# The first loads in another order, the last sums begun from alpha x, and the register loads and branches around the expert pass moved

## The reference, cut to what matters

```python
q, k, v, z, xbc, dt = jnp.split(x @ w_in, IN_SPLITS, axis=-1)      # mixer; w_in is 1024 x 3080, dt its last 8 columns
x = _layer_norm(alpha * x + mixer(x), g, b)
x = _layer_norm(alpha * x + cross_attention(x, memory), g, b)
out = jnp.zeros_like(x)                                            # layer 1: _moe
for e in range(N_EXPERTS):
    out = out + _swiglu(x, w_exp_gu[e], w_exp_down[e]) * gate[..., e:e + 1]
x = _layer_norm(alpha * x + out, g, b)                             # the last norm; its x is the output
```

## Time and profile before

| what | value |
|---|---|
| time, median of 3 runs | 1843.98 us (1843.71 to 1846.29) |
| the profiled execution's own time | 1844.95 us |
| its span | 1843.2 us |
| PE busy | 1783.9 us, 97% of the span |
| DVE, ACT, POOL busy | 1223.8, 853.3, 100.2 us |
| granted TensorE clock, mean | 0.988 |
| bytes moved, mean rate | 454.10 MB, 246 GB/s |

### The profile page before, as it was taken

How to read it: one execution, slowest core, us unless ns; L and a number is a source line. 1 busy time by engine, 2 the same in 40 slices (tenths; PEclk the granted TensorE clock), 3 DMA queues, 4 the chain that set the end, 5 groups by cost and what they waited for, 6 DMA issues and landing times.

```text
span 1843.2 us, 24556 instructions
## 1 busy us (share of the span) xinstructions
PE 1783.9 (97%) x9058; PEld 1399.0 (76%) x9058; DVE 1223.8 (66%) x1708; ACT 853.3 (46%) x978; POOL 100.2 (5%) x114
## 2 busy tenths in 40 slices
PE   7999999999999999999899999999999999999996
PEld 4646587799998565577688888888888888888884
DVE  2686526155544287534438889797988889897972
ACT  1122211054432131312126777776767777777752
POOL 0530000000000531000000000000000000000000
PEclk8999999999999999999999999999999999999998
DMA  9556545845426265543766899898999999998930
GB/s 322 173 195 217 212 170 196 283 150 181 168 99 220 102 221 177 213 186 134 268 201 205 301 314 381 293 368 308 354 345 323 358 317 368 308 375 299 362 158 26
DMA packets 298982, 454.10 MB, mean 246 GB/s; under 512 B 10710, under 2 KB 213648, under 8 KB 298886
## 3 DMA queue, kind: packets, MB, share of 16 engines
q1 hardware_dynamic: 294022, 440.47, 69.6%
q0 software_dynamic: 2576, 8.38, 1.5%
q10 hardware_dynamic: 2304, 4.20, 0.6%
HBM read 440.77 MB, written 12.38 MB: 246 GB/s over the span
## 4 chain that ended last, share of the span: by engine, by line
PE 87%; DVE 6%; ACT 4%; issue 1%; SPq 1%; DMA 1%; ACTq 0%; POOL 0%; DVEq 0%
PE bank L1147 85%; PE bank L1151 2%; DVE arena L2591 1%; DVE ring_low L2074 1%; ACT high L1702 1%; ACT L1702 0%; ACT arena L1765 0%; DVE R L2205 0%; ACT xT L1801 0%; DMA out<-mem_rows 0%; ACT ye_high L1738 0%; ACT SQ L1786 0%; DVE st L2563 0%; SPq L717 0%; SPq L723 0%
## 5 line engine op out<-in xcount | busy, mean ns | idle before, releaser
L2074 DVE TENSOR_TENSOR ring_low<-ring,high 128x2048 fp32r<-128x2048 f32 x264 | 602.8, 2290 | 93.7 <-ACT high L1702 85.5
L1702 ACT ACTIVATE high<-ring 128x2048 fp32r<-128x2048 f32 x264 | 505.6, 1918 | 107.1 <-PE bank L1147 106.1
L1147 PE MATMUL bank<-high,xg_high 128*128 128x512 f32 x704 | 281.8, 400 | 7.3 <-DVE ring_low L2074 7.0
L1147 PE MATMUL bank<-ring_low,xg_high 128*128 128x512 f32 x704 | 275.1, 391 | 0.0
L1147 PE MATMUL bank<-high,xg_low 128*128 128x512 f32 x704 | 274.3, 390 | 0.0
L1147 PEld LDWEIGHTS bank<-high,xg_high 128*128 128x128 f32 x704 | 132.2, 188 | 34.0 <-DVE ring_low L2074 8.4
L1147 PEld LDWEIGHTS bank<-ring_low,xg_high 128*128 128x128 f32 x704 | 132.1, 188 | 28.6
L1147 PEld LDWEIGHTS bank<-high,xg_low 128*128 128x128 f32 x704 | 132.5, 188 | 25.2
L1765 ACT ACTIVATE arena<-bank 128x512 f32<-128x512 f32 (+3 forms) x95 | 46.3, 525 | 212.5 <-PE bank L1147 142.9
L1147 PE MATMUL bank<-high,he_high 128*128 128x512 f32 x352 | 139.7, 397 | 0.0
L1147 PE MATMUL bank<-ring_low,he_high 128*128 128x512 f32 x352 | 137.4, 390 | 0.0
(11 more groups left out here) (320 smaller groups left out, 2583.1 us busy)
## 6 DMA issues: line engine op xcount, KB each, us to landing
ring<-in_w_exp_gu SPq DMA_DIRECT2D x176, 1024.0 KB, 11.3
ring<-in_w_exp_down SPq DMA_DIRECT2D x40, 2048.0 KB, 14.0
ring<-in_w_in SPq DMA_DIRECT2D x12, 2048.0 KB, 11.3
ring<-in_w_ffn_gu SPq DMA_DIRECT2D x22, 1024.0 KB, 7.9
ring<-in_w_ckv SPq DMA_DIRECT2D x8, 2048.0 KB, 9.3
ring<-in_cache_mem_k SPq DMA_DIRECT2D x16, 1024.0 KB, 8.1
ring<-in_cache_mem_v SPq DMA_DIRECT2D x16, 1024.0 KB, 6.7
ring<-in_cache_attn_k SPq DMA_DIRECT2D x32, 256.0 KB, 4.1
```

Source lines behind the costliest of these rows:

```text
L1147: return M.matmul(out, lhsT, rhs, start=start, stop=stop)
L1702: S.activation(high_bufs[h % HIGH_BUFS][:], ring[:, s, j * HALF:(j + 1) * HALF], ACT.Copy).then_inc(split_high, 1)
L2074: V.tensor_tensor(ring_low[:, s, part], ring[:, s, part], high_bufs[h % HIGH_BUFS][:], ALU.subtract).then_inc(split_low, 1)
```

## The change

**Start, loads.** SP issues the identity alone, x, then layer 0's q weights; behind these the rest of `const`, the six vectors, the memory rows and the page table. The nine small loads go to POOL's queue, behind its memsets. In the ring, the memory's slot now stands behind q's.

**Start, compute.** PE transposes only x before q's tiles; two of the five x groups go to ACT. The dt product stands behind q's second tile (tile 0) in both layers; the transposes of vectors and memory behind q's last tile in layer 0. `vraw` moves to the end of `arena`. DVE's copies of the vectors stand behind the dt arithmetic.

**Around the expert pass.** The register load of `cnti` stands ahead of pass 0 on PE, ACT, DVE and SP. The test for pass 2 stands inside the test for pass 1. `acc` starts from alpha times `xT` (POOL, 8 operations, after `xT` is final) and not from zero; `R = alpha*xT + acc` and `moe_done` are gone. The last norm's sums read `acc`, each block k after its last addition. `last_scatter` ends in 6 warm products and not 19, and uses banks 2 and 3 in place of 6 and 7.

**The end.** SP stores `y_tok` in three parts, each as soon as ACT has copied it; POOL no longer stores outputs.

```diff
 def ring_chunks():
-    c = [(("x",), 2, "pe", ("xin", 4)), (("mem",), 1, "pe", ("mem", 3))]
+    c = [(("x",), 2, "pe", ("xin", 4))]
     for l in range(L):
-        c += [((l, n), 1, "pe", (l, "tok", n, DECODE_FIRST[-1])) for n in ("q", "k")]
+        c += [((l, "q"), 1, "pe", (l, "tok", "q", DECODE_FIRST[-1]))]
+        if l == 0:
+            c += [(("mem",), 1, "pe", ("mem", 3))]
+        c += [((l, "k"), 1, "pe", (l, "tok", "k", DECODE_FIRST[-1]))]
...
         def _(sp):
-            sp.dma_start(const[:], a["consts"]).then_inc(const_landed, 16)
+            sp.dma_start(const[:, C_ID:C_ID + P], a["consts"][:, C_ID:C_ID + P]).then_inc(ident_landed, 16)
...
                 columns((l, "q"), w_in, 0)
                 if l == 0:
+                    first_vectors()
+                    memory_rows()
...
-            stream_experts(0)
             sp.wait_ge(pos_known, 1)
             most = sp.value_load(cnti[0:1, 0:1], min_val=0, max_val=T)
+            stream_experts(0)
...
+            for t in range(2):
+                copied(sp, ("out", 2 * t + 1))
+                sp.dma_start(y_p[0, t * P:(t + 1) * P, :], y_tok[:, t, :]).then_inc(y_stored, 16)
+            copied(sp, ("out", 5))
+            sp.dma_start(y_s[:, 0, :], y_tok[0:8, 2, :]).then_inc(y_stored, 16)
+            sp.wait_ge(y_stored, 16 * 3)
...
         def _(pool):
+            for n in range(L):
+                pool.dma_start(wdt[:, n], a["w_in"][n, :, 3072:3080].rearrange("(k p) n -> p k n", p=P)
+                               ).then_inc(small_landed, 16)
...
+                    xT_act.wait(pool, l, 13)
+                    xT_dve.wait(pool, l, 1)
                     for k in range(KT):
-                        G.memset(acc[:, k, :], 0.0).then_inc(part_added, 1)
+                        G.tensor_scalar(acc[:, k, :], xT[:, k, :], ALPHA, None, ALU.mult).then_inc(part_added, 1)
...
             def last_scatter(c):
-                warm(T_BANKS[0], 5)
-                result_ready(EXPERTS, c)
                 pe.wait_ge(xg_taken, (2 * EXPERTS + 2) * (c + 1))
                 pe.wait_ge(xg_low_ready, (2 * EXPERTS + 2) * (c + 1))
+                warm(X_BANKS[0], 5)
+                result_ready(EXPERTS, c)
...
-                warm(T_BANKS[0], 19)
+                warm(X_BANKS[0], 6)
...
-            one_pass(0)
             pe.wait_ge(pos_known, 1)
             most = pe.value_load(cnti[0:1, 0:1], min_val=0, max_val=T)
-            for c in range(1, passes):
-                with pe.If(most > (0 if always else lots * c)):
-                    one_pass(c)
+            one_pass(0)
+
+            def more_passes(c):
+                if c < passes:
+                    with pe.If(most > (0 if always else lots * c)):
+                        one_pass(c)
+                        pe.wait_ge(part_added, parts_before(EXPERTS + 1, c))
+                        more_passes(c + 1)
...
-                        last = mm(bk[:, 0:T], mean_of, R[:, k, :], k == 0, k == KT - 1)
+                        else:
+                            pe.wait_ge(part_added, parts_before(EXPERTS, 0) + k + 1)
+                        last = mm(bk[:, 0:T], mean_of, (R if part else acc)[:, k, :], k == 0, k == KT - 1)
...
-                        if first:
+                        if c == "q" and t == DECODE_FIRST[1]:
                             pe.wait_ge(small_landed, 16 * 9)
...
+                    if l == 0 and c == "q":
+                        vector_columns()
+                        memory_columns()
...
                     dve.wait_ge(part_added, parts_before(EXPERTS + 1, 0))
-                    V.scalar_tensor_tensor(R[:], xT[:], ALPHA, acc, ALU.mult, ALU.add).then_inc(moe_done, 1)
-                    dve.wait_ge(moe_done, 1)
                     norm(l, 2, None)
```

More of the change, by code:

```diff
@@ L188, in psum_groups @@
 def psum_groups():
-    g = [(("vec",), "V")]
-    g += [(("xin", n), "V") for n in range(5)] + [(("mem", n), "A") for n in range(4)]
+    g = [(("xin", n), "A" if n in (1, 3) else "V") for n in range(5)]
     for l in range(L):
@@ L198, in psum_groups @@
                 add("V" if t == 2 else "A", "tok", c, t)
-                if c == "q" and t == DECODE_FIRST[0]:
+                if c == "q" and t == DECODE_FIRST[1]:
                     add("V", "dt")
+                if l == 0 and c == "q" and t == DECODE_FIRST[-1]:
+                    g += [(("vec",), "V")] + [(("mem", n), "A") for n in range(4)]
         add("V", "acs")
@@ L1748, in expert_activations, with more_passes @@
             xT_dve.wait(act, L - 1, 1)
-            one_pass(0)
             act.wait_ge(pos_known, 1)
             most = act.value_load(cnti[0:1, 0:1], min_val=0, max_val=T)
-            for c in range(1, passes):
-                with act.If(most > (0 if always else lots * c)):
-                    one_pass(c)
+            one_pass(0)
+            def more_passes(c):
+                if c < passes:
+                    with act.If(most > (0 if always else lots * c)):
+                        one_pass(c)
+                        more_passes(c + 1)
+            more_passes(1)
         @block.scalar
@@ L1805, in _ @@
             S.preload_act_table_set(EXP_AND_LN)
-            for n in range(4):
-                copy_out(("mem", n), memT[:, 4 * (n % 2):4 * (n % 2) + 4, (n // 2) * P:(n // 2 + 1) * P],
+            for n in (1, 3):
+                copy_out(("xin", n), xT[:, 4:8, (n // 2) * P:(n // 2 + 1) * P],
                          lambda bk: bk[:].rearrange("p (k n) -> p k n", k=4))
@@ L1838, in _ @@
                             copy_out((l, "tok", name, t), qk_raw[:, t, 512 * c:512 * (c + 1)], lambda bk: bk[:])
+                    if l + c == 0:
+                        for n in range(4):
+                            copy_out(("mem", n), memT[:, 4 * (n % 2):4 * (n % 2) + 4, (n // 2) * P:(n // 2 + 1) * P],
+                                     lambda bk: bk[:].rearrange("p (k n) -> p k n", k=4))
                 decays_in.wait(act, l)
@@ L2144, in one_pass, with more_passes @@
                 last_scatter(c)
-            one_pass(0)
             dve.wait_ge(pos_known, 1)
             most = dve.value_load(cnti[0:1, 0:1], min_val=0, max_val=T)
-            for c in range(1, passes):
-                with dve.If(most > (0 if always else lots * c)):
-                    one_pass(c)
-                    dve.wait_ge(part_added, parts_before(EXPERTS + 1, c))
+            one_pass(0)
+            def more_passes(c):
+                if c < passes:
+                    with dve.If(most > (0 if always else lots * c)):
+                        one_pass(c)
+                        dve.wait_ge(part_added, parts_before(EXPERTS + 1, c))
+                        more_passes(c + 1)
+            more_passes(1)
         @block.vector
@@ L2227, in _ @@
             step.inc(V.memset(xs, 0.0))
-            bk = take(dve, ("vec",))
-            step.done(V.tensor_copy(pick[:], const[0:40, C_PICK:C_PICK + 8]))
-            step.inc(V.tensor_copy(vecT[:, 0, 0:122], bk[:, 0:122]))
-            emptied_after(("vec",), V.tensor_copy(vecT[:, 1, 0:64], bk[:, 128:192]))
-            for n in range(5):
+            for n in (0, 2, 4):
                 t, bk = n // 2, take(dve, ("xin", n))
@@ L2299, in _ @@
                 V.tensor_tensor(da, dtv, An[:, l, :], ALU.mult).then_inc(da_ready.sem, 1)
+                if l == 0:
+                    bk = take(dve, ("vec",))
+                    step.inc(V.tensor_copy(vecT[:, 0, 0:122], bk[:, 0:122]))
+                    emptied_after(("vec",), V.tensor_copy(vecT[:, 1, 0:64], bk[:, 128:192]))
+                    dve.wait_ge(const_landed, 16)
+                    step.done(V.tensor_copy(pick[:], const[0:40, C_PICK:C_PICK + 8]))
+                    for n in range(L):
+                        step.inc(V.tensor_scalar(col_attn(n), col_attn(n), 1.0 - LAM_INIT[n], None, ALU.mult))
                 other_quarters(1, "k", qk_raw[0:8, 2, 512:1024])
```

115 lines of the change are left out of this document (60 added, 55 removed).

## The result

The changed kernel takes 1831.36 us (median of 4 runs, 1830.35 to 1833.72), where the kernel before took 1843.85 beside it (1840.45 to 1846.29): 0.9936 of it, 95% interval 0.9921 to 0.9951. A second time it was 1829.42 against 1843.09, 0.9930 (0.9915 to 0.9945). So the change gains 12.5 to 13.7 us, where 22.9 were forecast. The range ended at 1831: the first median lies just beyond it, the second inside.

A forecast was written before the change was run, and what follows sets the result against it. PE was taken to bound the kernel, carrying 87% of the chain that ended last. Start -4.7, middle +1.0, end -14.4 and stores -4.8 sum to -22.9 on 1844.95: 1822.0, or 1821 on the median's scale, range 1814 to 1831.

The forecast's parts named there:

- Start: Program begin to `acs`: q's weights issued earlier, `acs` at 56.1 and not 60.85, 4.7 us sooner; bounds 9.2 sooner to 0.8 later.
- q's landing: At the start: 3.6 MB at 389 GB/s take 9.3 us, so q's weights are there at 13.0, bounds 11.7 to 14.5.
- POOL's packets share the 16 DMA engines with q: Rival at the start, chance 0.17 (shared with a low clock): the start gives nothing, 1826 us.
- The other steps of the term: From q's tile to `acs`: PE's work is 45.4 us, 43.1 with two thirds of the clock loss staying; `acs` at 56.1.
- The small loads were there ahead of dt: At the start: POOL issues the nine by about 15.5, dt wants them at 24, 6 us to land, price nothing.
- Middle: Routing to the first expert: the register load delays the warm products and all behind them, 1.0 us later, bounds 0 to 4.3.
- The register load: On PE between routing and the warm products: 0.9 us by the old rows, moving the gather and first expert later.
- POOL's products: Eight alpha products ahead of routing: 0.6 us each, ending at 960.7, memsets at 961.9, just ahead of the routing's 962.16.
- The mechanism: Rival at the routing, chance 0.06: at 1.04 us each POOL's products end at 965.5 and cost 3.3 us, 1824.
- The stretch up to the routing: From `acs` to the transposes ahead of the routing: no change forecast, 0 us.
- End: Last scatter to the mean's end: fewer warm products, one branch, sixteen matmuls at full clock; 14.4 us sooner, bounds 8.4 to 15.2.
- Stores: After the mean: SP stores outputs early, only 32 KB remain, no late POOL drain; 4.8 us sooner, bounds 3.5 to 5.8.

The follow-up runs named there:

- loads_on_sync: The changed kernel with the nine small loads moved from GpSimd's queue to SyncE's, behind the memory rows and ahead of k: 1824.59 us against 1845.01 before.
- all_behind_q: The changed kernel with SyncE and GpSimd both waiting for q's landing before issuing anything behind it: 1829.76 us against 1845.01 before.
- end_alone: The kernel before with only the change's later parts (register loads, nested branch, alpha products, sums, stores) and the old start: 1828.22 us against 1845.01 before.
- loads_before_mem: loads_on_sync with small loads ahead of the memory rows, memsets ahead of POOL's products, PE's register load behind the expert loop: 1820.50 us against 1844.17 before.

## Why the prediction was wrong

**Start: wrong, -4.7 forecast, +0.2 measured.** The step that failed is q's landing. POOL's small loads were priced by their bytes: 0.4 MB among 3.6 MB at 389 GB/s. Beside them the full engines moved less, 151 GB/s at the worst, and q's landing fell behind by more than this lost rate (2.1 of 5.7 us); 2.3 us went when nothing stood behind q. That put q at 18.36, outside the bounds of 11.7 to 14.5. The upper bound should have held a case in which these loads slow q. Such a case stood among the rivals, "POOL's packets share the 16 DMA engines with q", at 0.17 and priced at the whole term, 4.7; it was the one that came. A stretch of the kernel before could have warned, columns as above; its small loads were being issued then:

```profile
18.00:20.00 2.00, 1.40 (x12) 0.61 (x16) 0.00 (x0) 0.00 (x0) 0.00 (x0) 0.86 0.73 107
```

The engines were busy for 0.73 of it and moved 107 GB/s. The other steps of the term held: with q in time (loads_on_sync) the tile began at 12.63 and `acs` at 55.33, against 13.0 and 56.1. From q's tile to `acs` the changed kernel takes 42.67 us, forecast 43.1; so close a figure is partly luck, since it is 41.4 to 44.3 in the other kernels with the new start (all_behind_q apart), and with the old start 42.24 before and 39.93 in end_alone. The small loads were there ahead of dt, as forecast.

**Middle: sign right, size wrong, +1.0 forecast, +3.1 measured, inside its bounds of 0 to 4.3.** The register load was put at 0.9 and cost 1.0 to 1.1 (1.57 of idling for 0.49), and a loss of clock, 0.9 here, was left out. POOL's products were mis-sized: 0.6 us each was taken, 0.84 measured (6.75 for eight). So the memset that the routing waits for came at 968.02, not just ahead of PE's logits but 1.9 us behind them. The mechanism was named as a rival with 3.3 us at 1.04 each; its measured price is 1.0, or 1.9 with the clock.

**The stretch up to the routing: nothing forecast, +4.0 measured.** The range took one trace's 892.47 for fixed. It is not: other traces stand from 890.16 to 896.51.

**End: right, -14.4 forecast, -14.2 measured.** One branch begun at 1807.7 and 3.90 long, over at 1811.6. The forecast's 1804.2, moved by the 7.4 us by which the last scatter came later, is 1811.6. The sixteen matmuls ran at full clock in 3.81. The fourteen other traces with one branch have 3.32 to 3.76 us. The Trainium skill's 108 ns (Advanced Engine Details and Errata, "Control Flow Timing") is again far from what a jump over a whole pass costs here.

**Stores: right, -4.8 forecast, -4.5 measured.** Copy to span's end fell by 5.6, and 1.1 was given back in the last transposes and copies: the granted clock was 0.50 from 1827.0 to 1829.1 us, and 1.00 at the same place before.

As a sum: 22.9 forecast; the start's 4.9 and the middle's 2.1 did not come, and the unforeseen stretch cost 4.0. The medians differ by 1.3 more than the profiled executions, since that of the changed kernel stands 2.4 above its median and that of before 1.1. The start alone would have left the forecast at 1826, inside the range; this took one rival at a time and left out the upper corner of its own bounds, 1837, and here three misses came together. With the start and the middle mended, loads_before_mem has 23.7 us.

## What to carry over

Do not price small loads on a second queue by their bytes; put them behind the transfer that matters, on its own queue: moving nine loads of 0.4 MB brought q's tile 5.7 us sooner. When an engine gets more work ahead of something that others wait for, put the old part first: three memsets ahead of eight products gave back what the products had cost the routing. A register load hides where the sequencer runs ahead of a full array, and shows where it follows a wait.

## What was not expected of the hardware

- The same nine loads delayed q by 2.7 us from ScalarE's queue and by 5.7 to 6.0 from GpSimd's (8 to 10 us: 314 and 151 GB/s); on ScalarE's they were issued 1.3 us sooner and landed 6.9 later.
- POOL needs 0.84 us for a product of 128 x 264, where DVE's operation of that shape in the earlier trace rows took 0.36.
- A branch of PE's sequencer over a whole pass takes 3.3 to 3.9 us in all fifteen traces with one branch; a register load takes 0.49 on the sequencer and 1.0 to 1.1 on the path (1.57 of idling for 0.49).
